# Gate and up products of a two-block transformer kernel: one 512-column stream over the rows' head and rest, and a sum of two blocks on VectorE

## The reference, cut to what matters

```python
def swiglu(h, w_gate_up, w_down):
    gate, up = jnp.split(h @ w_gate_up, 2, axis=-1)
    return (jax.nn.silu(gate) * up) @ w_down

D_FF = 2816
# second block, the same form:
    a, b = jnp.split(hn @ w_in, 2, axis=-1)
    y = (jax.nn.silu(a) * b) @ w_out
```

## Time and profile before

| | |
|---|---|
| median of 3 runs | 1650.65 us |
| the profiled execution, its own time | 1652.22 us |
| its span from first to last instruction | 1650.4 us |
| TensorE (PE) matmuls | 1614.3 us busy, 98%, 10737 matmuls |
| VectorE (DVE) | 980.3 us, 59% |
| ScalarE (ACT) | 827.2 us, 50% |
| GpSimd (POOL) | 148.6 us, 9% |
| DMA, 16 engines | 60.1% of their time for the weights, 187 GB/s |

### The profile page before, as it was taken

One profiled execution on the slowest core, in us unless ns is written; L12 is line 12 of the kernel. 1 busy time (PEld: TensorE's weight loads), 2 busy tenths in 40 slices (PEclk: granted clock), 3 DMA queues, 4 the chain that ended last, 5 costly groups with the idle time before them and its releaser, 6 DMA issues.

```text
span 1650.4 us, 25510 instructions
## 1 busy us (share of the span) xinstructions
PE 1614.3 (98%) x10737; PEld 1442.6 (87%) x10737; DVE 980.3 (59%) x1652; ACT 827.2 (50%) x1188; POOL 148.6 (9%) x141
## 2 busy tenths in 40 slices
PE   7999999999999999999999999999999999999997
PEld 6888899987879989998899999889888888789986
DVE  5686744445635575446665666567747876564444
ACT  4565543434569754444454464444545546354442
POOL 1210010100002200101001100001000000001000
PEclk9999999999999999999999999999999999999999
DMA  9756866777653355556555676598572565575552
GB/s 322 245 198 224 268 225 225 242 251 244 217 195 103 123 188 187 180 179 217 191 171 171 195 147 186 179 190 166 138 152 70 133 168 175 180 236 183 184 167 88
DMA packets 224417, 309.46 MB, mean 188 GB/s; under 512 B 5004, under 2 KB 146720, under 8 KB 224304
## 3 DMA queue, kind: packets, MB, share of 16 engines
q1 hardware_dynamic: 222064, 301.29, 60.1%
q0 software_dynamic: 1664, 5.84, 1.0%
q10 hardware_dynamic: 576, 0.71, 0.1%
HBM read 306.77 MB, written 1.05 MB: 187 GB/s over the span
## 4 chain that ended last, share of the span: by engine, by line
PE 88%; DVE 6%; ACT 4%; issue 1%; DMA 0%; POOL 0%; DVEq 0%; ACTq 0%
PE ps L144 85%; PE ps L147 2%; DVE wl L157 2%; DVE SM L167 1%; DVE MT L167 1%; ACT wh L153 1%; ACT L153 1%; ACT SA L153 1%; DVE X L167 0%; ACT FT L153 0%; DVE MT L164 0%; DMA X<-in_x_dram 0%; ACT MT L153 0%; DVE SM L163 0%; DVE SA L167 0%
## 5 line engine op out<-in xcount | busy, mean ns | idle before, releaser
L157 DVE TENSOR_TENSOR wl<-raw,wh 128x1024 fp32r<-128x1024 f32 x498 | 606.6, 1258 | 407.1 <-ACT wh L153 406.3
L153 ACT ACTIVATE wh<-raw 128x1024 fp32r<-128x1024 f32 x498 | 502.0, 1053 | 231.1 <-PE ps L144 105.2
L144 PE MATMUL ps<-XTH,wh 128*128 128x256 f32 x1792 | 512.1, 286 | 4.9 <-issue 3.6
L144 PE MATMUL ps<-XTH,wl 128*128 128x256 f32 x1792 | 504.3, 281 | 0.6 <-DVE wl L157 0.6
L144 PE MATMUL ps<-XTL,wh 128*128 128x256 f32 x1792 | 504.2, 281 | 0.0
L144 PEld LDWEIGHTS ps<-XTH,wh 128*128 128x128 f32 x1792 | 339.6, 190 | 17.4 <-issue 8.8
L144 PEld LDWEIGHTS ps<-XTL,wh 128*128 128x128 f32 x1792 | 339.5, 189 | 2.8 <-issue 2.4
L144 PEld LDWEIGHTS ps<-XTH,wl 128*128 128x128 f32 x1792 | 339.4, 189 | 0.8 <-DVE wl L157 0.8
L144 PE MATMUL ps<-wh,XTH 128*128 128x512 f32 x352 | 143.3, 407 | 0.0
L144 PE MATMUL ps<-wl,XTH 128*128 128x512 f32 x352 | 139.0, 395 | 0.0
L144 PE MATMUL ps<-wh,XTL 128*128 128x512 f32 x352 | 139.0, 395 | 0.0
(11 more groups left out here) (295 smaller groups left out, 1972.1 us busy)
## 6 DMA issues: line engine op xcount, KB each, us to landing
raw<-in_w_ffn_in_dram SPq DMA_DIRECT2D x66, 1024.0 KB, 5.1
raw<-in_ffn_w_gate_up_dram SPq DMA_DIRECT2D x44, 1024.0 KB, 5.1
raw<-in_w_in_dram SPq DMA_DIRECT2D x40, 1024.0 KB, 8.5
raw<-in_w_ada_dram SPq DMA_DIRECT2D x36, 1024.0 KB, 5.8
raw<-in_w_ffn_out_dram SPq DMA_DIRECT2D x30, 1024.0 KB, 5.1
raw<-in_ffn_w_down_dram SPq DMA_DIRECT2D x20, 1024.0 KB, 5.1
raw<-in_a_w_qkv_dram SPq DMA_DIRECT2D x12, 1024.0 KB, 7.4
raw<-in_kv_w_dram SPq DMA_DIRECT2D x8, 1024.0 KB, 5.8
```

The costliest lines, as they stand in the source:

```text
L144: return NOTHING if self.e is None else self.e.matmul(o, l, r, start=start, stop=stop, skip_group_check=skip)
L153: return self.e.activation(o, i, fn, bias=bias, scale=scale)
L157: return NOTHING if self.e is None else self.e.tensor_tensor(o, a, b, f)
```

## The change

The rows' head and rest become one tensor (XT, XU) with an axis for the two, at the same addresses. A new product `paired` replaces `stationary` in `hidden` alone: for each block k one matmul streams head and rest (512 columns in two runs of 256) over the same block of `wh`, into a whole bank, and one matmul streams the head's 256 columns over the block of `wl` into the bank's first half. The two blocks f lie in two banks, a pair. The bank's first half and second half must still be added: VectorE does that with a tensor_reduce over both banks, 1024 elements in and 512 out, for gate into SG and for up into the temp. ScalarE's Silu then works on SG in place, and VectorE's multiply reads two SBUF tiles.

```diff
+        PP = [ctx.enter_context(nc.psum_tensor(f"ps{i}", [P, 2, 512], F32)) for i in range(4)]
+        PS = [PP[i // 2][:, i % 2, :] for i in range(8)]
...
+        def pair_sums(*key):
+            return PP[BANK.get(key, 0) // 2][:, :, :].rearrange("p f (z t) -> p f t z", z=2)
...
+            def take_pair(*key):
+                order = {b: i + 8 * any(sig is a_small for sig, _ in frees) for i, (b, frees) in enumerate(free)}
+                _, b = min((max(order[b], order[b + 1]), b) for b in (0, 2, 4, 6) if b in order and b + 1 in order)
+                for z, frees in free:
+                    for sig, what in frees if z // 2 == b // 2 else ():
+                        pe.wait_ge(*sig.at(*what))
+                free[:] = [f for f in free if f[0] // 2 != b // 2]
+                BANK[key] = b
+                return PP[b // 2]
...
+            def paired(key, wt, n0, XX, ready):
+                o = take_pair(*key)
+                _, gs = booked.pop(key, None) or piece(wsrc(wt, 0, 8, n0, 256), 8, 256)
+                for f in range(2):
+                    both = o[:, f, :].rearrange("p (z t) -> p z t", z=2)
+                    for i, g in enumerate(gs):
+                        hh = WH[g % NHL][:, :].rearrange("p (k n) -> p k n", k=4)
+                        ll = rest_half(g).rearrange("p (k n) -> p k n", k=4)
+                        for kk in range(4):
+                            k = 4 * i + kk
+                            a, b = hh[:, kk, f * P:f * P + P], ll[:, kk, f * P:f * P + P]
+                            pe.wait_ge(*ready(k))
+                            pe.wait_ge(*cast.at(g))
+                            pe.mm(both, a, XX[:, :, k, :], k == 0, k == 7, True)
+                            pe.wait_ge(*rest.at(g))
+                            m = pe.mm(o[:, f, 0:T], b, XX[:, 0, k, :], False, k == 7, True)
+                        if f == 1:
+                            m.then_inc(*consumed.up(g))
...
-            def hidden(name, w_in, XH, XL, ready, pairs):
+            def hidden(name, w_in, XX, ready, pairs):
                 for c in pairs:
-                    stationary((name, "g", c), w_in, 256 * c, XH, XL, ready)
-                    give((name, "g", c), a_out, name, "sg", c)
+                    paired((name, "g", c), w_in, 256 * c, XX, ready)
+                    give_pair((name, "g", c), v_out, name, "gs", c)
...
-                    act.wait_ge(*done(name, "g", c))
-                    if c > pairs[0]:
-                        act.wait_ge(*v_out.at(name, c - 1))
-                    act.act(SGt[:, :], ps(name, "g", c)[:, :], ACT.Silu).then_inc(*a_out.up(name, "sg", c))
+                    act.wait_ge(*v_out.at(name, "gs", c))
+                    act.act(SGt[:, :], SGt[:, :], ACT.Silu).then_inc(*a_out.up(name, "sg", c))
...
             def hidden(name, SGt, temps, pairs):
                 for c in pairs:
+                    tm = temps[c % 2][:, :]
+                    dve.wait_ge(*done(name, "g", c))
+                    dve.red(two(SGt[:, :]), pair_sums(name, "g", c), ALU.add).then_inc(*v_out.up(name, "gs", c))
                     yield
                     dve.wait_ge(*done(name, "u", c))
-                    dve.wait_ge(*a_out.at(name, "sg", c))
                     if c >= pairs[0] + 2:
                         dve.wait_ge(*g_out.at(name, "hl", c - 2))
-                    dve.tt(temps[c % 2][:, :], ps(name, "u", c)[:, :], SGt[:, :], ALU.mult).then_inc(*v_out.up(name, c))
+                    dve.red(two(tm), pair_sums(name, "u", c), ALU.add).then_inc(*v_out.up(name, "us", c))
+                    dve.wait_ge(*v_out.at(name, "us", c))
+                    dve.wait_ge(*a_out.at(name, "sg", c))
+                    dve.tt(tm, tm, SGt[:, :], ALU.mult).then_inc(*v_out.up(name, c))
```

More of the change, by code:

```diff
@@ L237, in program @@
         xt0 = fixed.o
-        XTH = fixed("XTH", [P, 8, T], F32R)
-        XTL = fixed("XTL", [P, 8, T], F32R)
+        XT = fixed("XT", [P, 2, 8, T], F32R)
+        XTH, XTL = XT[:, 0, :, :], XT[:, 1, :, :]
         C = fixed("C", [P, CK])
@@ L269, in program @@
         XC = c_("XC", [P, 2, D])
-        XUH = c_("XUH", [P, 8, T], F32R)
-        XUL = c_("XUL", [P, 8, T], F32R)
+        XU = c_("XU", [P, 2, 8, T], F32R)
+        XUH, XUL = XU[:, 0, :, :], XU[:, 1, :, :]
         r2 = c_.o
@@ L315, in program @@
         WS = g_("WS", [P, 4, P])
-        PS = [ctx.enter_context(nc.psum_tensor(f"ps{i}", [P, 512], F32)) for i in range(8)]
+        PP = [ctx.enter_context(nc.psum_tensor(f"ps{i}", [P, 2, 512], F32)) for i in range(4)]
+        PS = [PP[i // 2][:, i % 2, :] for i in range(8)]
         every = []
@@ L428, in take, with give_pair @@
                 return PS[b]
+            def take_pair(*key):
[7 more added lines that the diff above has]
+                return PP[b // 2]
+            def give_pair(key, sig, *what):
+                free.extend((BANK[key] + z, ((sig, what),)) for z in range(2))
             def give(key, sig, *what):
@@ L506, in stationary @@
                 look_ahead()
+            def paired(key, wt, n0, XX, ready):
[16 more added lines that the diff above has]
+                            m.then_inc(*consumed.up(g))
+                            used.add(g)
+                GROUP[key] = gs[-1]
+                look_ahead()
             def moving(key, wt, row, n, kts, o, XH, XL, nk, ready):
@@ L551, in rows @@
                     yield 0
-            def hidden(name, w_in, XH, XL, ready, pairs):
+            def hidden(name, w_in, XX, ready, pairs):
                 for c in pairs:
-                    stationary((name, "g", c), w_in, 256 * c, XH, XL, ready)
-                    give((name, "g", c), a_out, name, "sg", c)
+                    paired((name, "g", c), w_in, 256 * c, XX, ready)
+                    give_pair((name, "g", c), v_out, name, "gs", c)
                     yield 0
-                    stationary((name, "u", c), w_in, DFF + 256 * c, XH, XL, ready)
-                    give((name, "u", c), v_out, name, c)
+                    paired((name, "u", c), w_in, DFF + 256 * c, XX, ready)
+                    give_pair((name, "u", c), v_out, name, "us", c)
                     yield 0
@@ L722, in block1_ffn @@
                 yield "gap", 1
-                for _ in hidden(n, I["ffn_w_gate_up"][layer], XTH, XTL, half_ready(n), range(11)):
+                for _ in hidden(n, I["ffn_w_gate_up"][layer], XT, half_ready(n), range(11)):
                     yield 0 if layer else ("side", "gates")
@@ L737, in block2_ffn @@
                 own_first[0] = False
-                for q, _ in enumerate(hidden(n, w_in, XTH, XTL, half_ready(n), range(11))):
+                for q, _ in enumerate(hidden(n, w_in, XT, half_ready(n), range(11))):
                     if q in GATE_PE:
@@ L1002, in ctx_main @@
                     n = f"d{h0}"
-                    for q, _ in enumerate(hidden(n, I["w_ffn1_in_2"][0], XUH, XUL, half_ready("c1"),
+                    for q, _ in enumerate(hidden(n, I["w_ffn1_in_2"][0], XU, half_ready("c1"),
                                                  range(h0 // 2, h1 // 2))):
```

## The result

The changed kernel takes 1686.32 us (median of 4 runs, 1685.23 to 1687.23) where the kernel before took 1650.58 us beside it: 35.7 us more, a ratio of 1.0216 with a 95% interval of 1.0203 to 1.0229. The forecast was 1640 us with a range of 1632 to 1655. The profiled execution took 1685.23 us, with a span of 1683.2.

The account below looks back on a forecast made before the run. The prediction took PE's pace, or a wait put in front of PE, as the bound. 17.5 us of gain less 4.5 and 1.5 us of waits made 11.5 us less, forecast 1640 us, range 1632 to 1655.

Parts of the forecast that it names:

- DVE's work: On DVE: 110 added reductions at 1.22 us each, 134 us more work, 980 to 1114 us.
- the pace in f1: On PE: 344 to 347 ns from fused matmul to fused matmul, products of 5.5 us.
- the plain stages at no cost: Pure feed-forward stages: the reductions' delays of 1.2 us are covered by 11 us of look-ahead, cost nothing.
- rival 2: All fused products: a matmul has next to no fixed cost, so the gain is 2.3 us, time 1654 us; chance 0.06.
- the mechanism beside the second attention: d8's six products: Silu waits for DVE's rest and reduction, delaying exponentials and masks PE needs; 4.5 us lost.
- the same delay seen earlier: Up product at 549 us: its wait for the pair a reduction holds until 550.5, not counted again.
- the gain: On PE, over 110 products: fused matmuls save 17.5 us, 625.8 us down to 608.3.
- The middle of 5.67 us: Kernel before, 88 products outside f1: time per product, taken as the middle of 5.63 and 5.70 us.
- The first attention has more room on ACT, and the starts of f0 and l have chains of the same kind; I put 1.5 us on them together: First attention, starts of f0 and l: waits of 1.5 us together, between 0 and 5.
- given back at least one whole product earlier: Banks in all products: a free pair is nearly always that old, except for the up product at 549 us.
- Rival 3: Beside both attentions: 16 context products each put 1.5 us of queue waits before PE, 24 us, 1657 us; chance 0.15.
- Rivals 1 and 4: All products: 1, slower pace of 233.3 ns, 1650 us, chance 0.20; 4, whole gain, waits absorbed, 1633 us, chance 0.07.

Follow-up runs that it names:

- plain_stages: Kernel before, with fused products, pairs and reductions only where the feed-forward has PE to itself (f0 from group 4, f1 from 1, l from 2): 1643.69 us, 0.9965.
- unfused: Changed kernel with each 512-column matmul split again into two of 256, pairs and reductions kept: 1695.18 us, 1.0279.
- own_first: Changed kernel with DVE's reduction and multiply ahead of the two wl subtractions where PE doesn't need a piece's rest at once: 1652.45 us, 1.0015.
- no_add: Changed kernel without the reductions; Silu and multiply read each bank's first block, fused stream and pairs stay: 1646.33 us, 0.9979.
- pass_only: Kernel before with its three matmuls and single banks, plus DVE's added reduction pass in the changed kernel's order: 1687.53 us, 1.0236.
- before_own: Kernel before with DVE's multiply ahead of the two wl subtractions in gate and up steps; no reductions, fusion or pairs: 1648.42 us, 0.9988.

## Why the prediction was wrong, by its steps

**What held.** PE's pace bounds the plain stages, DVE's work (1.22 us a reduction, 980 to 1107.8 us), the pace in f1 (346.7 ns a step; 344 to 347 was named), the plain stages at no cost (plain_stages, and rival 2 falls with unfused), and in part the mechanism beside the second attention. 4.5 us were put there and the trace has 6.7, but the near match is partly luck: 1.11 and 2.06 us of it are PE waiting for a pair that a reduction holds, which the prediction took for the same delay seen earlier, and only the waits for SA (1.6, 0.6 before) and OA (2.5, 0.5 before) are those that it named. The rows of the changed kernel that answer to the fourth and fifth group of before, one for the reductions into SG and one for f1 (stretch, length, then busy PE, PEld, DVE, ACT and POOL, clock, DMA share, GB/s):

```profile
L183 DVE TENSOR_REDUCE SG<-ps 128x512 f32<-128x1024 f32 x55 | 66.8, 1215 | 2.2 <-PE ps L144 2.2
```

```profile
633.00:766.50 133.50, 131.15 (x737) 114.56 (x736) 95.49 (x90) 61.06 (x77) 14.25 (x11) 0.99 0.55 181
```

The idle time of 2.2 us before all 55 reductions says it at a glance: the product is nearly always done before DVE comes to it, and its banks wait for DVE.

**A term mis-sized: the gain.** 17.5 us were named, 11 to 12 were there. f1 gave 0.21 us a product, as reckoned (0.23). The other 88 products gave less than the 0.14 reckoned: 0.08 in the ten measured here, some 0.11 in f0 and l, which gave back 2.4 and 2.5 us over their 22 products. The middle of 5.67 us in the kernel before was taken between two short stretches, and the ten had 5.63.

**The step that failed: "The first attention has more room on ACT, and the starts of f0 and l have chains of the same kind; I put 1.5 us on them together".** The delay was reckoned from ACT's load, and so only where ACT was full. But the queue that matters is DVE's. At the places shown, where two streams mix, it stands idle for wh and then does two subtractions before the step's own work. That was read correctly beside the second attention ("only when DVE has finished the rest and the reduction") and not carried to the others, nor to e, which has the context's convolution beside it. Outside the second attention the measured cost is 39.7 us, with the half clock. own_first takes 34 us away by DVE's order alone.

**Its companion: a pair "given back at least one whole product earlier", at no cost.** That compares PE's order, not the time at which the reader is done. At 141 us DVE had 1.78 us of standing still, 2.36 of subtractions and 1.22 of reduction between it and the pair's release; 14.6 us of waits are for banks held this way. no_add shows the pairs' own part, two waits of 5.6 us and the clock; pass_only shows that with eight banks the waits only come elsewhere.

**A term that was missing: the clock.** 10.5 us. Each of the five new waits over 3 us was followed by matmuls at 1.2 GHz, and so were two of the five between 2 and 3 us. The kernel before has two such stretches in its trace, and I did not look at what a pause would bring.

**The rivals.** Rival 3 had the right mechanism and sign and, with 24 us on 16 products, half the size, because it kept to the two attentions. Its condition of 1.1 us a product was far exceeded in d0, where two places alone cost 15.1 us. Rivals 1 and 4 did not occur: the pace was the faster one, and the waits were not absorbed.

## What to carry to other kernels

Work that is put on an engine with 40% idle time is not covered by it: ask where in that engine's queue it stands, what the instruction ahead of it waits for, and which buffer it now holds; then try it ahead of that instruction before judging the idea. A buffer's age in the producer's order says nothing of when its reader is done. Put a price on the clock for new waits of TensorE too (here nothing for 0.78 us, about 1.5 us in one of three cases for 2.79, 2.3 us each for 7.19), and use a cheaper form only in the stages where no other stream shares the queues.

## What the runs showed of the hardware that was not expected

**DVE's and GpSimd's subtractions take longer side by side.** In own_first and before_own a wl subtraction takes 1346 and 1339 ns in the mean, in the kernels before and changed 1258 and 1259. DVE of own_first in f1:

```profile
656.87 2.35 DVE L157 TENSOR_TENSOR wl<-raw,wh 128x1024 fp32r<-128x1024 f32 x2
...
663.14 3.46 DVE L157 TENSOR_TENSOR wl<-raw,wh 128x1024 fp32r<-128x1024 f32 x2
...
674.23 3.46 DVE L157 TENSOR_TENSOR wl<-raw,wh 128x1024 fp32r<-128x1024 f32 x2
```

and its GpSimd:

```profile
663.97 1.56 POOL L157 TENSOR_TENSOR HTL<-MT,HTH 128x512 fp32r<-128x512 f32 x1 [9.54 <-ACT HTH L153]
```

The pair of subtractions that has GpSimd's beside it takes 3.46 us, the pair without takes 2.35, and GpSimd's takes 1.56 us where it takes 1.30 alone. All read two tiles of SBUF. The Trainium skill, "VectorE: DVE Perf Modes", section "Two Vector instructions with no wait between them", notes that the read interface for DVE's second SBUF input is shared with GpSimd; the rows agree with that, though no run here varied it. The multiply from PSUM beside it was not measured.

**A fused matmul with two runs of columns** takes 229 ns to the next start and its 256-column partner 118, the means over 343 of each in f1. Two runs of 256 columns, 32 bytes past a multiple of 64, stand 2 ns over the faster of the 512-column rows and 4 under the slower.
